# Feed forwards: the fourth sum of weight quarters made by an adding transfer issued by GpSimd, in place of the second sum

## What is computed

```python
D_MODEL = 1024; SEQ = 512; D_FF = 2816; DEPTH = 2
def swiglu(h, w_in, w_out):
    gate, up = jnp.split(h @ w_in, 2, axis=-1)
    return (jax.nn.silu(gate) * up) @ w_out
# layers of the first kind, DEPTH times
h = layer_norm(DEEPNORM_ALPHA * h + 0.5 * swiglu(h, ffa_w_in[i], ffa_w_out[i]), ...)
h = layer_norm(DEEPNORM_ALPHA * h + mix, ...)
h = layer_norm(DEEPNORM_ALPHA * h + 0.5 * swiglu(h, ffb_w_in[i], ffb_w_out[i]), ...)
# layer of the second kind, once: two feed forwards around its mixer
def swiglu_2(h, w_gate, w_up, w_down):
    return (jax.nn.silu(h @ w_gate) * (h @ w_up)) @ w_down
```

## Time and profile before

| | |
|---|---|
| median of 2 runs | 3495.95 us |
| span of the profiled execution, first to last instruction | 3490.0 us |
| the median less that span | 5.95 us |
| TensorE (PE) busy | 3305.1 us, 95% |
| VectorE (DVE) busy | 2335.2 us, 67% |
| ScalarE (ACT) busy | 1581.0 us, 45% |
| GpSimd (POOL) busy | 483.0 us, 14% |
| data moved by DMA | 327.38 MB, mean 94 GB/s |

### The profile page before, as it was taken

One profiled execution on the slowest core, in us unless ns is written; L12 is line 12 of the kernel. 1 busy time (PEld: TensorE's weight loads), 2 busy tenths in 40 slices (PEclk: granted clock), 3 DMA queues, 4 the chain that ended last, 5 costly groups with the idle time before them and its releaser, 6 DMA issues. The chain is left out here.

```text
span 3490.0 us, 59574 instructions
## 1 busy us (share of the span) xinstructions
PE 3305.1 (95%) x24514; PEld 2821.9 (81%) x24514; DVE 2335.2 (67%) x3196; ACT 1581.0 (45%) x2553; POOL 483.0 (14%) x399
## 2 busy tenths in 40 slices
PE   8999998899999999999998899999999989989998
PEld 8998775778998699986767689986899856669986
DVE  7877475548875488764845488755887258758852
ACT  5552435236552355524352365524655254645541
POOL 0003113540003000031135300030000100300001
PEclk9999999999999999999999999999999999999999
DMA  4235220012235223452200123342333222122331
GB/s 159 100 132 189 74 67 32 4 50 97 98 133 167 75 105 103 136 178 74 67 26 4 50 97 109 134 157 74 127 109 112 82 68 73 43 85 86 109 108 61
DMA packets 81590, 327.38 MB, mean 94 GB/s; under 512 B 11905, under 2 KB 11905, under 8 KB 65833
## 3 DMA queue, kind: packets, MB, share of 16 engines
q1 hardware_dynamic: 81320, 323.57, 27.4%
HBM read 321.15 MB, written 4.74 MB: 93 GB/s over the span
## 5 line engine op out<-in xcount | busy, mean ns | idle before, releaser
L236 DVE TENSOR_TENSOR w_low<-w_raw,w_high 128x1024 fp32r<-128x1024 f32 (+1 forms) x241 | 340.1, 1412 | 441.4 <-ACT w_high L228 440.5
L228 ACT ACTIVATE w_high<-w_raw 128x1024 fp32r<-128x1024 f32 (+1 forms) x241 | 284.6, 1183 | 526.6 <-PE ffa_ps L254 170.6
L834 DVE TENSOR_TENSOR w_low<-w_raw,w_high 128x1024 fp32r<-128x1024 f32 (+1 forms) x186 | 220.9, 1188 | 21.4 <-ACT w_high L713 10.7
L713 ACT ACTIVATE w_high<-w_raw 128x1024 fp32r<-128x1024 f32 (+1 forms) x186 | 190.3, 1023 | 3.0 <-PE ffa_ps L254 1.6
L252 PE MATMUL mix_proj_ps<-mix_x_high,w_high 128*128 128x512 f32 x416 | 169.7, 408 | 13.1 <-DVE mix_x_low L401 13.0
L254 PE MATMUL mix_proj_ps<-mix_x_high,w_low 128*128 128x512 f32 x416 | 166.5, 400 | 0.0
L253 PE MATMUL mix_proj_ps<-mix_x_low,w_high 128*128 128x512 f32 x416 | 165.5, 398 | 0.0
L252 PE MATMUL ffa_ps<-ffa_hid_high,w_high 128*128 128x512 f32 x352 | 141.4, 402 | 0.5 <-DVE w_low L236 0.5
L252 PE MATMUL b_f_ps<-b_f_hid_high,w_high 128*128 128x512 f32 x352 | 139.6, 397 | 0.5 <-DVE w_low L236 0.5
L253 PE MATMUL b_f_ps<-b_f_hid_low,w_high 128*128 128x512 f32 x352 | 139.2, 396 | 0.0
L254 PE MATMUL b_f_ps<-b_f_hid_high,w_low 128*128 128x512 f32 x352 | 139.2, 395 | 0.0
(11 more groups left out here) (748 smaller groups left out, 10942.2 us busy)
## 6 DMA issues: line engine op xcount, KB each, us to landing
ffa_quarters<-in_ffa_seven SPq DMA_DIRECT2D x40, 1024.0 KB, 4.8
ffb_quarters<-in_ffb_seven SPq DMA_DIRECT2D x40, 1024.0 KB, 4.8
b_f_quarters<-in_ffn_seven SPq DMA_DIRECT2D x40, 1024.0 KB, 5.0
w_raw<-in_mix_in SPq DMA_DIRECT2D x77, 512.0 KB, 3.4
w_raw<-in_ffa_out SPq DMA_DIRECT2D x32, 704.0 KB, 5.7
w_raw<-in_ffb_out SPq DMA_DIRECT2D x32, 704.0 KB, 5.4
w_raw<-in_ffn_out SPq DMA_DIRECT2D x32, 704.0 KB, 4.1
ffa_ada_raw<-in_w_ada SPq DMA_DIRECT2D x80, 256.0 KB, 2.9
```

What stands on the lines that cost most here:

```text
L228: act.activation(self.high[:, self.place(n, 0, kt)], self.raw[:, n % SLOTS, :kt * P], ACT.Copy).then_inc(self.rounded, 1)
L236: dve.tensor_tensor(self.low[:, whole], self.raw[:, n % SLOTS, :kt * P], self.high[:, whole].bitcast(F32), ALU.subtract).then_inc(self.spl ...
L713: act.activation(ops.split(group, r)[0], ops.source(group, r), ACT.Copy).then_inc(part_rounded, 1)
L834: dve.tensor_tensor(low, ops.source(group, r), high.bitcast(F32), ALU.subtract).then_inc(part_split, 1)
```

## The change

The fourth sum is no longer written to a place of its own. The second sum of round r goes to half r % 2 of `s24`. When group g2 of round r has been split, the second sum has been used, and GpSimd issues a transfer that adds quarter 2 of the block to it in place (`accum_op=ALU.add`, from SBUF to SBUF, 128x512 float32, 256 KB). What then stands in half r % 2 is the fourth sum. The second sum of round r+1 goes into the other half. `add_fourth` goes from VectorE. Its place in the semaphore `sum_made` goes too (`SUMS`), and two semaphores `fourth_made` tell that a transfer has landed. ScalarE waits for it ahead of rounding g2 of round r+1, and SP ahead of loading the buffer whose quarter 2 the transfer read. The products s2 and s4 find their weights in half r % 2 as well.

```diff
+        self.fourth_made = [sem(f"w_fourth_made{j}") for j in range(2)]
+        self.fourths = 0
...
 SUMS = numbers([("s13", 0), ("s2", 0)]
-               + [(n, r + ahead) for r in range(SEVEN) for n, ahead in (("s13", 1), ("s4", 0), ("s2", 1)) if r + ahead < SEVEN])
+               + [(n, r + ahead) for r in range(SEVEN) for n, ahead in (("s13", 1), ("s2", 1)) if r + ahead < SEVEN])
...
+    fourth_made, fourths = ws.fourth_made, ws.fourths
+    ws.fourths += SEVEN // 2
...
+    def second(self, r):
+        return self.s24[:, r % 2 * HALF_COLUMNS:(r % 2 + 1) * HALF_COLUMNS]
...
         if name in ("s4", "s2"):
-            at = (2 if name == "s2" else 3) * HALF_COLUMNS
+            at = (2 + r % 2) * HALF_COLUMNS
...
             def _(pool):
                 halves.gpsimd(pool)
+                for r in range(SEVEN):
+                    pool.wait_ge(part_split, SPLITS["g2", r])
+                    pool.dma_start(ops.second(r), ops.part(r, 2, 3), accum_op=ALU.add).then_inc(fourth_made[r % 2], 16)
                 finish.gpsimd(pool)
...
                     if r >= RAWS:
                         sp.wait_ge(part_split, SPLITS["g4", r - RAWS])
+                        sp.wait_ge(fourth_made[(r - RAWS) % 2], 16 * (fourths + (r - RAWS) // 2 + 1))
                     sp.dma_start(ops.raw[:, r % RAWS, :], quarters[r]).then_inc(landed[r % RAWS], 16)
...
-                        act.wait_ge(sum_made, SUMS["s2", r + 1] if r + 1 < SEVEN else SUMS["s4", r])
+                        if r + 1 < SEVEN:
+                            act.wait_ge(sum_made, SUMS["s2", r + 1])
+                        act.wait_ge(fourth_made[r % 2], 16 * (fourths + r // 2 + 1))
                         round_part("g2", r + 1)
...
                 def add_second(r):
-                    dve.wait_ge(sum_made, SUMS["s4", r - 1] if r > 0 else SUMS["s13", r])
+                    dve.wait_ge(sum_made, SUMS["s13", r])
                     if r > 0:
                         dve.wait_ge(part_split, SPLITS["g2", r - 1])
-                    dve.tensor_tensor(ops.s24[:, 0:HALF_COLUMNS], ops.s13[:, 0:HALF_COLUMNS], ops.part(r, 1, 2), ALU.add)\
+                    dve.tensor_tensor(ops.second(r), ops.s13[:, 0:HALF_COLUMNS], ops.part(r, 1, 2), ALU.add)\
                         .then_inc(sum_made, 1)
-                def add_fourth(r):
-                    dve.wait_ge(sum_made, SUMS["s2", r])
-                    dve.wait_ge(part_split, SPLITS["g2", r])
-                    dve.tensor_tensor(ops.s24[:, HALF_COLUMNS:], ops.s24[:, 0:HALF_COLUMNS], ops.part(r, 2, 3), ALU.add)\
-                        .then_inc(sum_made, 1)
...
                         add_ends(r + 1)
-                    if r < SEVEN:
-                        add_fourth(r)
                     if r + 1 < SEVEN:
                         add_second(r + 1)
```

## The result

The changed kernel takes 3529.88 us (median of 2 runs, 3529.76 and 3530.00) against 3495.95: 1.0097 times the time before, 95% interval 1.0081 to 1.0114. It is slower by 34 us, where 2.9 us faster was forecast. Its profiled execution has a span of 3528.1 us, 38.1 more than the one before.

The account below looks back on a forecast made before the run. TensorE was taken to bound settled rounds, with the transfer hidden. The profiled span of 3490.0 us less 2.9 of TensorE's waits gave 3487.1, plus 5.95 to the median: 3493.1 us, range 3487 to 3590.

Parts of the forecast that it names:

- What bounds a settled round: Settled rounds: TensorE waits for nobody, VectorE has 1.7 us to spare, so the removed addition gains 0 there.
- VectorE's part: One 128x512 addition of 685 ns less per round, 82 us over 120 rounds; gain only where VectorE is behind.
- the gain in sight: Start of feed forwards: TensorE's waits of 0.69, 0.70, 0.71 and three of 0.27 us vanish, 2.9 us in all.
- The loop and its limit: Split of g2, transfer, rounding, next split: hidden up to 7.72 us; above it each of 120 rounds pays the excess.
- L: Time from the end of g2's split to the transfer's landing, taken as 5.2 us, bounded by 2.3 and 9.2.
- the term of 0.8 us for sharing: Adding transfer beside the load: half of what 704 KB loads lose beside 1 MB of loads, 5.7 against 4.1 us.
- my upper bound: Adding transfer: load of quarters served first (4.8), then the transfer (3.4), plus GpSimd's part (1.04): 9.2 us.
- hidden: Forecast case: matmuls hide the transfer; own range 3488 to 3501 us; chance 0.71, including the last rival.
- the rival that came: Chain from split to rounding: the loop of transfers becomes the bound, up to 178 us slower, 3674 us; chance 0.15.
- GpSimd and VectorE in each other's way: GpSimd prepares transfers only while VectorE rests, 192 us slower, 3688 us; or VectorE slows by 0.73 us; chance 0.05.
- my 4.4: Adding transfer without sharing: 3.4 us as for 512 KB plus 1.04 for GpSimd; the skill's estimate was 3.6 us.
- The last rival: Transfers hold back the loads of quarters; even 5 us more is hidden, 3493 us; chance counted within the 0.71.

Follow-up runs that it names:

- run 1: Changed kernel, with SP issuing the load of quarters only when the adding transfer in flight has landed: 3492.37 us, ratio 0.9987 to the kernel before.
- run 9: Changed kernel, with SP's load of quarters also waiting for VectorE's sum c22, about 2.0 us later: 3492.81 us, ratio 0.9994 to the kernel before.
- run 4: Changed kernel, with GpSimd making the fourth sum by an addition instruction of its own, no transfer: 3498.70 us, ratio 1.0006 to the kernel before.
- Runs 5 to 7: Changed kernel with half the load behind the transfer (3491.77 us); with the load in four pieces (3490.68 us); with only 256 of 512 columns added (3493.24 us).
- run 2: Changed kernel, with GpSimd's transfer a plain copy over the second sum, the fourth sum left out: 3494.12 us, ratio 0.9989 to the kernel before.

## Why the prediction was wrong

- **What bounds a settled round** was read rightly: TensorE, with VectorE's idle time growing and nothing gained (10.03 and 10.08 us in run 1 as before).
- **VectorE's part** was right: 79.6 us of work gone (82 forecast, from 685 ns each), and in the changed kernel the waits of 0.7 us at the start of the feed forwards are gone. I had counted them in three; the trace before has them in five, and a fourth of the small gaps. So the gain in sight was 4.7 us (3.69 in five waits, 1.03 in four gaps), not 2.9. Where the loss is taken away, the medians lie 3.8 us (run 1) and 2.0 us (run 9) below before, of that size; of the two, only run 1's interval is clear of no change. The largest of the waits before:

```profile
3166.16 0.19 PEld L596 LDWEIGHTS b_f_ps<-b_f_token_sums,w_high 128*128 128x128 f32 x1 [0.89 <-DVE w_low L834]
```

- **The loop and its limit** were right, and they are what explains the loss: L + 2.31 for a round, free up to 7.72. In the round shown, the part that the prediction had to know beforehand, 2.31 us from rounding to split, is met to the hundredth.
- **The failed step is the term of 0.8 us for sharing**, "half of what 704 KB loads lose beside 1 MB of other loads". I had L = 3.4 + 1.04 + 0.8 = 5.2. Alone the transfer takes 0.3 us to reach GpSimd and 3.3 to land, 3.6 in all where I had 4.4. Beside the load it takes 0.3 + 7.4 = 7.7, so sharing is 4.1 us, five times my term, and L is at its limit of 7.72 where I had 2.5 us left. The error was in the row I chose: there all transfers are plain and stand in one queue. I argued with bytes, and the order of arrival decided. I had noted that the load "starts 0.6 us after the same split" and counted it for the rival, but the load "served first", which I had kept for my upper bound, was the case that came true in all 102 rounds beside a load. The bound itself, L = 9.2, is near the longest measured, 9.7; the median, 7.8, is far below it, as the transfer begins when 104 of the load's 144 packets have begun and does not wait for its landing.
- **The chances** were off by this: 0.71 on hidden, 0.15 on the rival that came. The size of the rival was taken from its end (178 us); over the 102 rounds with a load beside, the mean L is 8.02 us, just past the limit, which costs 34 us. That the time lies within my range of 3487 to 3590 says nothing for the forecast: the range was stretched upwards for this rival, and a gain was forecast where there is a loss.
- **GpSimd and VectorE in each other's way** did not happen with the transfer (685 ns for L901). The Trainium skill ("SBUF — State Buffer", Who interferes with whom) says that VectorE instructions with two SBUF inputs conflict with GpSimd's reads, not with its writes, and infers that preparing a transfer does not meet them. The traces agree: with the first in run 4 (1.78 us for 0.69), with the inference in the changed kernel (685 ns). The estimate of 3.6 us for the transfer alone, from the Trainium skill ("DMA: Bandwidth & Descriptors", Anatomy of one DMA), was better than my 4.4: measured are 3.6 us from the end of the split, 3.3 of them from the issue.
- **The last rival**, loads held back: the load did become 1.3 us slower, and that was hidden.

Left open: why transfers at the same 0.33 us distance from the load land anywhere from 7.1 to 9.3 us (it is not in when their first packet comes), and by which rule the engines hold a transfer from GpSimd until most of the piece of load in front of it has begun. Runs 5 to 7 show that the pieces of the load, and a little the transfer's own bytes, count once the load is first; run 2 does not show that the adding counts.

## What to carry to other kernels

A transfer that closes a loop from one round to the next has the round's length less the engines' part as its limit, and what goes beyond it is paid in every round. Price it beside what is issued within a microsecond of it, not by its own row, and look in the queues' packets which of the two came first. Where SP issues a large load just behind it, put the load behind the small transfer; here 0.66 us later was enough for the settled rounds, and one wait more on SP turned a 1% loss into a gain of a thousandth.

## What the hardware showed that I had not expected

- An adding transfer of 256 KB from SBUF to SBUF, issued by GpSimd: 0.86 us of issue, 3.3 us from issue to landing alone, 7.4 us (up to 9.3) with a 1 MB load issued 0.33 us behind it, 3.9 us with that load issued 1.0 us behind it (medians).
- With the load's first packet 0.14 us ahead of where the transfer's would come (1.29 against 1.43 us behind the issue), the transfer's first packet comes at 4.73 us, behind 104 of the 144 packets of the load, rows of 8 KB; with pieces of 4 and 2 KB rows it comes at 3.45 and 2.64 us, behind 106 and 94 of the first piece's 144.
- A plain copy of the same bytes from the same queue: 0.54 us of issue, 3.9 us beside the load issued 0.33 us behind it, with 80 packets against 144; 2.3 us with no load beside it. From SP, ahead of the load in its queue: 2.3 us.
- An addition of 128x512 on GpSimd beside VectorE: 1.67 us, and 1.67 us on the mean for the VectorE instruction of 0.69 us beside it.
